# Eleven dense pieces of the first two layers by seven products of quarters, with the orders written anew

## The reference

```python
h = x * (1.0 + scale[:, None, :]) + shift[:, None, :]
hc = ctx * (1.0 + scale_c) + shift_c
(a_q, a_k, a_v, a_g, g_q, g_k, g_v, g_af, g_ab, g_g,
 s_u, s_v, s_g, m_a, m_g, m_s) = jnp.split(h @ p['w_in'], pts, axis=-1)
(ca_q, ca_k, ...) = jnp.split(hc @ p['w_in'], pts, axis=-1)
...
y_attn = blocked_attention(ql, k_all, v_all) * jax.nn.silu(a_g)
...   # gated linear attention (scan), forward and backward, on g_q, g_k, g_v
y_gla = gla_finish(ol_f + flip(ol_b), p['gla_o_norm'], x.dtype) * jax.nn.silu(g_g)
y_sgu = sgu(s_u, s_v, ...) * jax.nn.silu(s_g)
...   # merge: gates sigmoid(m_a), sigmoid(m_g), sigmoid(m_s) on three branch products, then w_out
```

## Time and profile before

| | before |
|---|---|
| runs | 1558.76, 1561.94, 1564.1 us; median 1561.94 |
| the profiled execution | 1564.0 us, its span 1562.2 us |
| PE busy (records) | 1516.4 us, 97% (7888) |
| weight loads (PEld) | 1077.2 us, 69% |
| DVE, ACT, POOL busy | 681.1, 415.0, 281.9 us (44, 27, 18%) |
| DMA | 184.22 MB, mean 118 GB/s |
| loads of 2 MB | 69, median 8.3 us from issue to landing |
| layer 0 weave, merge, output | 24 to 402, 402 to 553, 553 to 653 us |
| layer 1 weave, rest | 655 to 925, 925 to 1013 us |
| the two layers of the second kind | 1013 to 1562 us |

### The profile page before, as it was taken

How to read it: one execution, slowest core, us unless ns; L and a number is a source line. 1 busy time by engine, 2 the same in 40 slices (tenths; PEclk the granted TensorE clock), 3 DMA queues, 4 the chain that set the end, 5 groups by cost and what they waited for, 6 DMA issues and landing times.

```text
span 1562.2 us, 19171 instructions
## 1 busy us (share of the span) xinstructions
PE 1516.4 (97%) x7888; PEld 1077.2 (69%) x7888; DVE 681.1 (44%) x1460; ACT 415.0 (27%) x814; POOL 281.9 (18%) x314
## 2 busy tenths in 40 slices
PE   6999999999999999999999999999999999999997
PEld 2544544455688885555877888588888758888873
DVE  1233433464633343523344311365687216568721
ACT  1122325232312210121235320134233213423320
POOL 0322210131455441113002102110100011010010
PEclk9999999999999999999999999999999999999999
DMA  8642222300122231322322243423221323332231
GB/s 362 262 175 108 108 108 108 135 27 17 65 81 81 97 123 68 150 108 97 119 108 108 102 156 120 175 102 144 109 110 71 147 115 149 126 112 106 88 128 40
DMA packets 17370, 184.22 MB, mean 118 GB/s; under 512 B 2306, under 2 KB 2818, under 8 KB 4740
## 3 DMA queue, kind: packets, MB, share of 16 engines
q1 hardware_dynamic: 17284, 183.01, 30.7%
HBM read 181.95 MB, written 1.05 MB: 117 GB/s over the span
## 4 chain that ended last, share of the span: by engine, by line
PE 89%; ACT 3%; DVE 3%; issue 2%; DMA 1%; POOL 1%; SPq 0%; POOLq 0%; ACTq 0%; DVEq 0%
PE ps L756 86%; PE ps L811 3%; DVE arena L1749 1%; DVE arena L1755 1%; DMA arena<-in_wf 1%; POOL arena L2362 1%; ACT arena L1333 1%; ACT L1709 0%; ACT L1707 0%; DVE arena L1752 0%; ACT arena L1577 0%; ACT arena L1707 0%; ACT arena L1593 0%; ACT L1595 0%; ACT L1593 0%
## 5 line engine op out<-in xcount | busy, mean ns | idle before, releaser
L756 PE MATMUL ps<-arena 128*128 128x256 f32 (+7 forms) x7396 | 1467.1, 383 | 33.8 <-DMA arena<-in_wf 12.3
L756 PEld LDWEIGHTS ps<-arena 128*128 128x128 f32 (+5 forms) x7396 | 1023.6, 178 | 445.4 <-issue 311.9
L2362 POOL TENSOR_TENSOR arena<-arena 128x256 f32<-128x256 f32 (+6 forms) x254 | 247.3, 994 | 825.8 <-DVE arena L1755 409.3
L1755 DVE SCALAR_TENSOR_TENSOR arena<-arena 128x256 f32<-128x256 f32 (+4 forms) x470 | 231.0, 545 | 143.4 <-ACT arena L1475 38.8
L1333 ACT ACTIVATE arena<-ps 128x512 f32<-128x512 f32 (+2 forms) x280 | 134.9, 505 | 448.3 <-PE ps L756 370.5
L1749 DVE TENSOR_TENSOR arena<-arena 128x512 f32<-128x512 f32 (+14 forms) x190 | 140.4, 761 | 170.9 <-ACT arena L1333 95.8
L1755 DVE SCALAR_TENSOR_TENSOR arena<-arena,ps 128x256 f32<-128x256 f32 (+2 forms) x121 | 54.0, 456 | 207.2 <-PE ps L756 96.9
L1749 DVE TENSOR_TENSOR arena<-ps,arena 128x512 f32<-128x512 f32 (+16 forms) x120 | 48.8, 434 | 106.0 <-PE ps L756 97.3
L811 PEld LDWEIGHTS ps<-arena 128*128 128x128 f32 x488 | 55.7, 141 | 29.4 <-issue 19.5
L811 PE MATMUL ps<-arena 128*128 128x128 f32 x488 | 71.5, 278 | 3.1 <-ACT arena L1611 1.5
L1752 DVE TENSOR_SCALAR arena<-arena 128x256 f32<-128x256 f32 (+9 forms) x181 | 62.8, 382 | 15.7 <-POOL arena L2362 10.8
(11 more groups left out here) (96 smaller groups left out, 294.4 us busy)
## 6 DMA issues: line engine op xcount, KB each, us to landing
arena<-in_wf SPq DMA_DIRECT2D x69, 2048.0 KB, 8.3
arena<-in_wf SPq DMA_DIRECT2D x22, 1024.0 KB, 6.5
arena<-in_wf SPq DMA_DIRECT2D x2, 1152.0 KB, 7.7
arena<-in_xinT SPq DMA_DIRECT2D x2, 1024.0 KB, 15.9
arena<-in_xin SPq DMA_DIRECT2D x4, 512.0 KB, 3.9
arena<-in_rp SPq DMA_DIRECT2D x2, 1024.0 KB, 8.2
arena<-in_consts SPq DMA_DIRECT2D x1, 1410.0 KB, 21.6
arena<-in_pa SPq DMA_DIRECT2D x2, 532.0 KB, 9.4
```

What stands on the lines that cost most here:

```text
L756: return e.matmul(o, l, r, start=start, stop=stop, skip_group_check=True)
L1755: return e.scalar_tensor_tensor(out=o, in0=x, scalar=s, in1=y, op0=op0, op1=op1)
L2362: return e.tensor_tensor(o, x, y, op)
```

## The change

Five pieces of layer 0 (`gqk`, `gv`, `ag`, `gg`, `su`) and six of layer 1 (`ag`, `gg`, `su`, `mg0`, `ms0`, `ma1`) are computed by the seven products of quarters. Their four dense steps become (1, 2), (6, 7), (5, 4), (3). Each product is 2 chunks of 4 k-tiles: 8 calls of `mm` with 256 moving columns in layer 0 and 128 in layer 1, in place of 32 calls with 512 or 256 for the whole piece. The weights' sums are made on DVE: 3 and 2 in a step `w1`, behind the dense step before the piece, where DVE first waits for the piece's landing; 1 and 4 in `w2`, in the piece's first step. The input's four sums are made once per layer. ACT copies products 1, 6, 7, 5 out (and 3, or a tanh of each quarter); DVE adds 2, 7 (kept in `EW`) and 7+4 from PSUM. Sums 1 of the weights go over the quarter w21; the others and the input's lie in units 4 to 6 of the ring, and in `X`. For that the ring has 4 units for pieces from `a0gqk` to `a0su`, and from `a1ag` to `a1ma1`. The adaLN rows use one buffer, not two. Waits of attention and scan for a chunk of `ag` or `gg` become waits for the whole piece. The two strings of `ORDER_A` are new.

```diff
+SEVEN = [[("gqk", "A"), ("gv", "A"), ("ag", "T"), ("gg", "T"), ("su", "A")],
+         [("ag", "T"), ("gg", "T"), ("su", "A"), ("mg0", "G"), ("ms0", "G"), ("ma1", "G")]]
...
 ORDER_A = [
-    "daadddddaddaddddadadgaaadgadgaadgdgaagdagadagadgadagadgagadgaadgadaaggadaaaggadggaadggagadgagdgaaddgaggadgggaa"
-    "dgagdagdagdggadgdgaadgaagadagaagdadgaadgadagddaadaaaddaaadaagagadgaaaggagadgagagagadgadaggdaggggg",
-    "addddddadddgdagagaddadddgadadgdgdadgdgadgagdadadggddadgadadadggagadgaddggagaadggdagdgaaddaggddaggdagggdgdaggda"
-    "ddagaddgadggadgdggaadgaggagdgagdggagagaggdadgaagddaddadggagdggdgdggddgdg"]
+    "ddaaadddddddddadaggdagdgdaggdgddaddagaggggdgaggadgadgadggaadagaaaadggaadgdaadagagagadgggdaaggagdggagdgaadggdaa"
+    "gdaggagaaggadagdaadaaggadaaagaaadaaadaaggaadgaadagaagdagdagaagdggadaadaadadaagdggaagadadadaddaggg",
+    "dddaddaddaddgdgadaaaadggddddadddaddggaddgdgddagaddagdaddaagggddggddgaggdadggagdgaagggdgaddagagaddggggaddagadgd"
+    "agdadgadgdgdgdggdgaggadgdaagdgadggagdagdaddggagaagggdadgaadaggagdgdagdgg"]
...
-    return steps + [[("m" + br + str(j), c, "A")] for br, j in EARLY[l] for c in range(4)]
+    steps += [[("m" + br + str(j), c, "A")] for br, j in EARLY[l] for c in range(4)]
+    for name, kind in SEVEN[l]:
+        i = [s[:1] for s in steps].index([(name, 0, "T" if kind == "T" else "A")])
+        for k in range(4):
+            steps[i + k] = [(name, x[0], "W" + kind) for x in WINOGRAD[2 * k:2 * k + 2]]
+        steps[i - 1] = steps[i - 1] + [("w1", name, "-")]
+        steps[i] = steps[i] + [("w2", name, "-")]
+    return steps
...
+        rest = Mem(arena, 4 * UNIT)
+        HW = [{n: rest.take(1024) for n in "1234"}]
+        WW = [{"2": r3(rest.take(1024), 4), "4": r3(rest.take(1024), 4), "3": r3(X[:, 1024:2048], 4)}]
+        assert rest.at <= NU * UNIT
+        rest = Mem(arena, 4 * UNIT)
+        HW.append({n: rest.take(512) for n in "1234"})
+        WW.append({n: r3(rest.take(1024), 4) for n in "234"})
+        EW = [X[:, 0:512], rest.take(256)]
...
+            done_with[f"rest{l}"] = dense_act(l, SEVEN[l][-1][0], 3)
         pieces, at, off, tenant, count = {}, 0, 0, [None] * NU, [0] * NU
+        short = [("a0gqk", "a0su"), ("a1ag", "a1ma1")]
+        ends = [0, 0]
+        rest_free = [None, None]
         for name, w in PLAN:
             k = -(-w // UNIT)
-            at = at if at + k <= NU else 0
+            for l in range(2):
+                if name == short[l][0]:
+                    rest_free[l] = [done_with[x] for x in tenant[4:] if x]
+                    tenant[4:], ends[l] = [f"rest{l}"] * 3, 4
+            units = max(ends) or NU
+            at = at if at + k <= units else 0
             count[at] += 16
             pieces[name] = (ring[:, at * UNIT:at * UNIT + w], wf[off:off + 128 * w].rearrange("(p n) -> p n", p=128),
                             (d_unit[at], count[at]), [done_with[x] for x in tenant[at:at + k] if x])
             tenant[at:at + k] = [name] * k
-            at, off = (at + k) % NU, off + 128 * w
+            at, off = (at + k) % units, off + 128 * w
+            for l in range(2):
+                if name == short[l][1]:
+                    ends[l] = 0
...
+            def one_of_seven(l, n, x):
+                w = use(f"a{l}{n}", 8)
+                _, s, t, _ = WINOGRAD[[y[0] for y in WINOGRAD].index(x)]
+                if x in (1, 2, 7):
+                    b = bank("dense", l, n, x)
+                else:
+                    b = psum("dense", l, n, 7 if x == 4 else 1)
+                    p.wait_ge(dense_act(l, n, {6: 1, 5: 6, 4: 7, 3: 5}[x]))
+                p.wait_ge(*(hk(l, kk)[0] for kk in range(8)), *(hk(l, kk)[1] for kk in range(8)))
+                if len(s) == 1:
+                    p.wait_ge(seven_sum(l, n, s))
+                if len(t) == 1:
+                    p.wait_ge(dense_dve(l, "hs", int(t) - 1))
+                W = quarter(w, 1, 2) if s == "1" else WW[l][s] if len(s) == 1 else quarter(w, s[1], s[0])
+                if len(t) == 1:
+                    H = r3(HW[l][t], 4) if l else halves(r3(HW[l][t], 4))
+                else:
+                    H = half_tokens(l, hT[:, 4 * int(t[0]) - 4:4 * int(t[0]), :], int(t[1]))
+                m = 128 if l else 256
+                for c in range(2):
+                    for k in range(4):
+                        w_c, h_c = (H[:, k, c], W[:, k]) if n == "gv" else (W[:, k, 128 * c:128 * c + 128], H[:, k])
+                        ins = mm(b[:, m * c:m * c + m], w_c, h_c, x in (1, 2, 7) and c == k == 0, k == 3)
+                return ins
...
+            def seven_weights(l, n, first):
+                k = [x for x, _ in SEVEN[l]].index(n)
+                name = f"a{l}{n}"
+                w11, w12, w21, w22 = (quarter(weights(name, 8), k, f) for f, k in ("11", "12", "21", "22"))
+                def make(s, x, y, op, product):
+                    if product:
+                        v.wait_ge(*([dense_done(l, SEVEN[l][k - 1][0], product)] if k else rest_free[l]))
+                    tt(w21 if s == "1" else WW[l][s], x, y, op).then_inc(dn_dve.hit(l, BY_DVE[l][(n, "w" + s)]), 1)
+                if first:
+                    v.wait_ge(pieces[name][2])
+                    make("3", w11, w21, ALU.subtract, 7)
+                    v.wait_ge(seven_sum(l, n, "3"))
+                    make("2", w22, WW[l]["3"], ALU.subtract, 6)
+                else:
+                    make("1", w21, w22, ALU.add, None)
+                    v.wait_ge(seven_sum(l, n, "2"))
+                    make("4", w12, WW[l]["2"], ALU.subtract, 3)
...
+            def seven_sums(l, n, x, kind):
+                if x == 1 and n == SEVEN[l][0][0]:
+                    for kk in range(8):
+                        v.wait_ge(*hk(l, kk))
+                    v.wait_ge(*rest_free[l])
+                    h11, h21, h12, h22 = (half_tokens(l, hT[:, 4 * k:4 * k + 4, :], t) for t in (1, 2) for k in range(2))
+                    o = {i: r3(y, 4) if l else halves(r3(y, 4)) for i, y in HW[l].items()}
+                    for i, (y, a1, a2) in enumerate(((o["1"], h12, h11), (o["2"], h22, o["1"]), (o["3"], h22, h12),
+                                                     (o["4"], h21, o["2"]))):
+                        if i in (1, 3):
+                            v.wait_ge(dense_dve(l, "hs", i // 2))
+                        tt(y, a1, a2, ALU.subtract).then_inc(dn_dve.hit(l, BY_DVE[l][("hs", i)]), 1)
+                def gated(f, t, src):
+                    q = f"{f}{t}"
+                    o = seven_result(l, n, f, t)
+                    v.wait_ge(dense_act(l, n, "t" + q if q != "12" else 3))
+                    stt(o, two_chunks(l, TH), 1.0, src or o, ALU.add, ALU.mult
+                        ).then_inc(dn_dve.hit(l, BY_DVE[l][(n, "g" + q)]), 1)
+                if x == 4 and kind == "WT":
+                    gated(2, 2, None)
+                if x in (2, 5, 4):
+                    f, t = {2: (1, 1), 5: (2, 2), 4: (2, 1)}[x]
+                    o = seven_result(l, n, f, t)
+                    b = two_chunks(l, EW[l] if x == 5 else psum("dense", l, n, 7 if x == 4 else 2), n)
+                    v.wait_ge(dense_done(l, n, x), dense_act(l, n, {2: 1, 5: 5, 4: 6}[x]))
+                    if n == "gqk" and x == 2:
+                        for c in range(2):
+                            ins = stt(o[:, c], b[:, c], 0.125, o[:, c], ALU.mult, ALU.add)
+                    else:
+                        ins = tt(o, b, o, ALU.add)
+                    ins.then_inc(dn_dve.hit(l, BY_DVE[l][(n, x)]), 1)
+                elif x == 7 and kind == "WT":
+                    gated(1, 1, None)
+                elif x == 3 and kind == "WT":
+                    gated(2, 1, None)
+                    gated(1, 2, two_chunks(l, psum("dense", l, n, 1)))
...
-                        v.wait_ge(at_v.at(l, w // 2), dense_dve(l, "ag", c))
+                        v.wait_ge(at_v.at(l, w // 2), dense_dve(l, "ag", "g12"))
...
-                        v.wait_ge(v.now(), dense_dve(l, "gg", 2 * hp + h))
+                        v.wait_ge(v.now(), dense_dve(l, "gg", "g12"))
```

More of the change, by code:

```diff
@@ L122, in dense_a, with act_events, dve_events @@
             steps += [[("mx", t, "V")] + ada()]
-    return steps + [[("m" + br + str(j), c, "A")] for br, j in EARLY[l] for c in range(4)]
+    steps += [[("m" + br + str(j), c, "A")] for br, j in EARLY[l] for c in range(4)]
[6 more added lines that the diff above has]
+    return steps
+def act_events(n, x, kind):
+    if kind[0] != "W":
+        return [(n, x)] if kind in "AT" else []
+    quarters = {7: ["t11"], 4: ["t22"], 3: ["t21"]}.get(x, []) if kind != "WA" else []
+    return ([(n, x)] if x in (1, 6, 7, 5) else []) + [(n, t) for t in quarters] + ([(n, 3)] if x == 3 else [])
+def dve_events(n, x, kind, first):
+    if n in ("w1", "w2"):
+        return [(x, "w" + s) for s in ("32" if n == "w1" else "14")]
+    if kind[0] != "W":
+        return [(n, x)] if kind in "TV" else []
```

(58 more changed lines are left out.)

56 lines of the change are left out of this document (46 added, 10 removed).

## The result

The changed kernel takes 1542.64 us (median of four runs, 1540.98 to 1544.69) where the kernel before takes 1561.29 (1558.76 to 1564.1): ratio 0.9882, 95% interval 0.9868 to 0.9897. Run again on another chip it came to 0.9880 (0.9864 to 0.9896). That is 18.7 us less. It is the time of the first rival, "all is covered" (1544).

The account below looks back on a forecast made before the run. The prediction took TensorE's own work, busy 97%, as the bound: 24.0 saved less 13.0 crossings, 3.3 clock and 2.0 misses gives 5.7 us less, 1558.3 profiled, 1556.2 as the runs' median; range 1544 to 1568.

Parts of the forecast that it names:

- the first rival: Layer 0's crossings: other steps cover all but gqk to gv; gain 18 us, 1544; chance 0.2, including half way to it.
- PE's 24.0 us: PE's products in both layers: seven-product pieces save 16.3 us in layer 0 and 7.7 in layer 1.
- rival 3: Layer 1: 128-wide records cost 0.124 us or more, 7.7 less gain, 1564; chance 0.15, shared with crossings at upper bounds.
- The sums of VectorE: Both weaves: some 42 us more DVE work in each, which fits as throughput and was costed at nothing.
- Rival 2: Both weaves: DVE's sums run slower beside GpSimd, 6 to 18 us slower than before, 1568 at half price; chance 0.2.
- gqk to gv: Layer 0 crossing: 4.1 us of work against a load landing after 8.6, so PE idles 4.5 us.
- gv to ag: Layer 0 crossing: level 1's products wait for scaled(1) behind w1, so PE idles 4.9 us (3.0 to 7.9).
- ag to gg: Layer 0 crossing: 6.0 us of work, none behind w1, so PE idles 2.6 us (0 to 3.6).
- gg to su: Layer 0 crossing: 8.2 us of work and a chain of copies behind the gating, 1.0 us idle (0 to 3).
- The new orders: Beyond the crossings: the same steps between the same pieces, a little denser, costed within the 2.0 us of misses.
- The misses, 2.0: Both weaves: products waiting where cover between copy and product is gone, 2.0 us in all (0 to 6).
- The clock: 3.3 us: Layer 0: a half-clock stretch of 1.65 us at each of two crossings idle over 4 us, 3.3 us.

Follow-up runs that it names:

- k9: The kernel before with the four-unit ring and the change's two order strings, without its products by seven and sums: 1568.3 us, ratio 1.0051.
- k6: The changed kernel with layer 0's scan step holding level 1's products moved ahead of ag's first product: 1552.87 us, ratio 0.9949.
- k7: The kernel before with the change's two order strings and nothing else: ratio 1.0008.
- k8: The kernel before with only the change's ring of four units, in the old orders: ratio 1.0155.
- k4: The changed kernel with no adaLN piece between gqk and gv, layer 0's later ones moved one crossing on, everything computed: 1546.46 us, ratio 0.9914.
- k5: The changed kernel with four more DVE additions of 128x1024 in each of the eleven pieces: 1557.33 us, ratio 0.9982.
- layer 1 alone: The changed kernel with only layer 1's six pieces by seven products, layer 0 as in the kernel before: 1553.85 us, ratio 0.9961.
- k3: The changed kernel without the load of a1ada0, whose products take gqk's weights, so gv loads a piece earlier: 1538.71 us, ratio 0.9874.
- k10: k4 with two light scan steps moved behind gv's first products and the last adaLN step beside sv2: 1540.2 us, ratio 0.9864.

## Why the prediction came out as it did

- **PE's 24.0 us.** Right. 512-wide records fell from 1120 to 800, 128-wide ones rose from 672 to 1344, and k9 against after leaves 22.7 to 23.4, within 3 us. Layer 1, priced by the 0.112 us of the earlier trace rows, gains 7.1 us in the trace and 6 alone; rival 3 is out.
- **The sums of VectorE.** Right, and for the reason given. In the weave of layer 0 (24 to 366 us, which holds all its sums) the additions cost what the earlier trace rows had, in layer 1 less:

```profile
L1927 DVE TENSOR_TENSOR arena<-arena 128x1024 f32<-128x1024 f32 x38 | 48.0, 1285 | 7.2 <-DMA arena<-in_wf 6.7 <-ACT arena L1633 0.3
...
L1927 DVE TENSOR_TENSOR arena<-arena 128x1024 f32<-128x1024 f32 x24 | 29.2, 1237 | 20.2 <-PE ps L850 20.0
```

The Trainium skill, "VectorE: DVE Perf Modes", in its section on the trn2 errata, has a formula for an fp32 addition; an estimate by it is 1224 ns at 1024 elements, and the trace agrees within 1 to 5%. Rival 2 did not occur, but its price was not idle: with the sums doubled, 15 of the 18.7 us are gone.
- **gqk to gv: 4.5 us and half clock.** The right total, 4.5 idle and a stretch at 0.50. Its working had one cause where there are two: 2.5 for the ring, 2.0 for a chain through DVE.
- **gv to ag: 4.9 us. This step failed**, and with it one of the two half-clock stretches. There is 0.5 us of idle time. I read the order string by one scan step too far: the table of the new order ahead of the prediction, and this term with its 13 steps, have level 1's products ahead of ag, with "g g a g g a"; the string has "g a g g a" there, 12 steps in all, and those products one dense step later, behind ag's products 1 and 2. PE reaches them at about 150.6 us, when DVE has long made scaled(1) (147.55) and copied level 0's products out. So ag waits for nothing but its transfer, and 7.9 us of work and 0.5 idle cover that. k6 moves the products where I had read them and gets idle time of the size that I forecast (5.96 for 4.9, within 3.0 to 7.9), at a cost of 10 us in all.
- **ag to gg 2.6 and gg to su 1.0: mis-sized**, for the first by a sizing from the light end. The steps in them last 8.6 and 10.2 us of work, where I had 6.0 and 8.2, at 0.32 and 0.6 us a step. And the load lands 8.0 to 8.1 us after its issue at all four crossings, not 8.6 (which is again the median from 120 to 400 us). The three crossings behind gv have between 7.9 and 10.2 us of work for it; the first of them is covered by 0.3 us only.
- **The new orders.** By themselves they are worth nothing (k7), and under the short ring they are worth some 15 us (k8, k9), in the crossings: k8 has five waits for a transfer, k9 has 3.6 and 0.2 us. My sum for the crossings, 13.0 + 3.3, was meant for the new order and is close to what the ring costs with the old one (17.6 idle, and its clock). The orders are the part of the change that pays for the ring, and I missed that by misreading one crossing and sizing the others too light, not by anything beyond these points.
- **The misses, 2.0.** None is seen. PE's idle time in layer 0's weave rose by 5.6 us (3.5 to 9.1), all of it within the crossings' 6.0, and layer 1 has none.
- **The clock: 3.3 us.** One stretch in the crossings in place of two. The crossing gqk to gv has its stretch of 3.4 us at 0.50; gv to ag, ag to gg and gg to su have none, with 0.5, 1.0 and no us idle. The Trainium skill, "TensorE: Matmul & The Clock Gate", in "Why this matters for your kernels", warns of longer idle gaps between bursts of matmuls, behind which the engine falls back to half rate; the trace agrees in so far as the three crossings without such a gap kept the full clock. That the engine was idle for 2.53 us at 584.92 in after and kept its full clock, where before fell to 0.50 after the same 2.53, no run here explains.
- **The sum.** Idle time of 5.6 us in place of 15.0 (13.0 and 2.0) and one half-clock stretch in place of two add 11.1 us to the 5.7: 16.8. The measured gain is 18.7. The 1.9 us that are left are no more than one or two of the stretches below, and that rival 1's 1544 was met within 1.4 us is luck to that extent. Its mechanism, though, is the one that the traces show: only gqk to gv shows.

## What to carry to other kernels

When a change brings a tighter resource and a new order of work together, price the resource under the new order, step by step from its own string, and not by the mean cost of a step: here the same ring costs 23 us in one order and 8.6 in the other. A stretch of work can be the cover of two things at once; taking it away because one of them is gone (k4) uncovers the other. And an engine busy for half of a weave is not free for twice its new work: in k5 layer 1 waits for sums although DVE is busy for 161 of 265 us; what counts is the time between two products that frame a sum.

## What the runs showed that I had not expected

Stretches of half clock of 3.4 or 6.8 us decide a part of every comparison of a few us in this kernel. Before had four of them ahead of the last few us of its span, after two, layer 1 alone none:

```profile
19.40:22.80 3.40, 3.40 (x5) 1.33 (x5) 0.51 (x2) 0.00 (x0) 0.00 (x0) 0.51 1.01 429
...
1220.90:1224.20 3.30, 3.30 (x10) 2.58 (x9) 0.46 (x1) 2.77 (x4) 0.00 (x0) 0.50 0.00 0
1490.60:1493.90 3.30, 3.30 (x8) 2.67 (x9) 0.00 (x0) 3.26 (x4) 0.00 (x0) 0.50 0.00 0
```

(Windows of before; the fourth is in the earlier trace rows.) Each is worth 1.7 us, so of the 19.3 us between the two profiled executions 3.4 are of this kind: three of before's four are absent in after (5.1 us), and the change brought one of its own (1.7). The runs that were only timed differ less: before's stand mostly at a clock of 0.997 and after's at 0.997 or 0.998, and a thousandth is 1.5 us of this span. A gain of 2 to 4 us that a trace shows plainly in its place, as in k3 and k10, can so be lost to a measurement of the whole.
